# Weight sums of the in-projection on VectorE, the first tap of the convolution on ScalarE

## The reference

```python
zxbcdt = h @ in_w                                   # 1024 -> 5184 columns
z   = zxbcdt[..., :D_INNER]
xbc = jax.nn.silu(centred_dwconv(zxbcdt[..., D_INNER:D_INNER + CONV_DIM], conv_w, conv_b))   # 5 taps
dt  = jax.nn.softplus(dt_raw + dt_bias)             # 64 columns, two directions
cum = jnp.cumsum(dt_c * a_neg, axis=2)              # then the chunked scan of both directions
y   = rmsnorm((y_f + flip(y_b) + xs * d_skip) * jax.nn.silu(z), norm_w)
out = y @ out_w
```

## Time and profile before

| | us |
|---|---|
| median of 3 runs (lowest, highest) | 1460.6 (1460.18, 1460.69) |
| profiled execution, its own time | 1461.46 |
| its span in the trace | 1459.7 |
| TensorE busy in the span | 1343.7 (92%) |
| VectorE, ScalarE, GpSimd busy | 680.5, 409.2, 275.3 |
| DMA moved | 338.78 MB, mean 232 GB/s |

### The profile page before, as it was taken

The page is one execution under the profiler, slowest core; times in us unless marked ns, Lnnn a source line. Parts: engine busy times, 40 slices in busy tenths (PEclk is TensorE's granted clock), DMA queues, the critical chain, the costliest instruction groups (busy, mean ns, idle before and its releaser), DMA issues.

```text
span 1459.7 us, 30536 instructions
## 1 busy us (share of the span) xinstructions
PE 1343.7 (92%) x12917; PEld 917.8 (63%) x12917; DVE 680.5 (47%) x1154; ACT 409.2 (28%) x1032; POOL 275.3 (19%) x258
## 2 busy tenths in 40 slices
PE   5988989998999799999999999999999989999876
PEld 2466766676667688755566556688757855565432
DVE  4585988767776865651222222152363532221112
ACT  2312244454545310221222222222152302221111
POOL 0322352535265600000111111000000001111100
PEclk9999999999999999999999999999999989999988
DMA  9754344334531641525999999876321289999993
GB/s 346 283 173 144 116 143 147 129 132 145 202 117 37 181 129 60 208 110 184 396 397 389 383 378 381 349 253 219 108 106 53 81 305 363 392 395 398 401 406 144
DMA packets 132222, 338.78 MB, mean 232 GB/s; under 512 B 13363, under 2 KB 63339, under 8 KB 125803
## 3 DMA queue, kind: packets, MB, share of 16 engines
q1 hardware_dynamic: 122571, 313.38, 58.8%
q0 software_dynamic: 6208, 12.60, 2.5%
q10 hardware_dynamic: 3296, 10.73, 2.0%
HBM read 327.88 MB, written 16.91 MB: 236 GB/s over the span
## 4 chain that ended last, share of the span: by engine, by line
PE 64%; DMA 8%; DVE 7%; SPq 4%; issue 4%; ACT 2%; POOL 1%; DVEq 0%; ACTq 0%; POOLq 0%
PE ps L1852 14%; PE ps L1475 9%; PE ps L1891 7%; PE ps L1722 6%; PE ps L1782 4%; SPq L673 3%; DMA tmp<-in_moe_w_up 2%; PE ps L2181 2%; PE ps L1913 2%; PE ps L2091 2%; PE ps L1395 2%; DMA ssb<-in_moe_w_down 1%; PE ps L1551 1%; SPq L675 1%; DMA tmp<-in_shared_w_down 1%
## 5 line engine op out<-in xcount | busy, mean ns | idle before, releaser
L1852 PE MATMUL ps<-ring,ssb 128*32 128x256 f32 x2368 | 138.3, 386 | 6.5 <-DMA ring<-in_moe_w_up 6.5
L2786 DVE COPY big<-ps 32x256 f32<-32x256 f32 x162 | 68.6, 423 | 145.7 <-PE ps L1891 144.0
L2777 DVE TENSOR_TENSOR ssb<-ssb,ps 128x128 f32<-128x128 f32 (+1 forms) x56 | 19.5, 348 | 247.9 <-ACT ssb L1199 247.9
L1852 PEld LDWEIGHTS ps<-ring,ssb 128*32 128x32 f32 x2368 | 80.7, 112 | 58.9 <-DMA ring<-in_moe_w_up 9.9
L1475 PE MATMUL ps<-hT,own 128*128 128x256 f32 x456 | 109.6, 389 | 2.7 <-POOL own L861 2.6
L1475 PEld LDWEIGHTS ps<-hT,own 128*128 128x128 f32 x456 | 85.2, 193 | 25.1 <-issue 14.1
L1212 ACT COPY big<-ps 32x256 f32<-32x256 f32 x162 | 58.6, 362 | 141.1 <-PE ps L1891 139.6
L1852 PE MATMUL ps<-tmp,ssb 128*32 128x256 f32 x1568 | 88.7, 379 | 4.8 <-DMA tmp<-in_moe_w_up 4.7
L1199 ACT ACTIVATE ssb<-ps 128x128 f32<-128x128 f32 (+1 forms) x56 | 18.2, 324 | 249.3 <-PE ps L1852 249.3
L936 POOL DMA_INDIRECT y_rows<-big,sidx x32 | 30.0, 938 | 304.9 <-DVE big L2786 304.1
L2367 DVE SCALAR_TENSOR_TENSOR ring<-ring,par 128x512 f32<-128x512 f32 x96 | 85.6, 892 | 3.4
(11 more groups left out here) (463 smaller groups left out, 2429.0 us busy)
## 6 DMA issues: line engine op xcount, KB each, us to landing
ring<-in_ada_w SPq DMA_DIRECT2D x44, 1024.0 KB, 5.0
ring<-in_moe_w_gate SPq DMA_DIRECT2D x60, 512.0 KB, 12.4
ring<-in_moe_w_up SPq DMA_DIRECT2D x60, 512.0 KB, 16.0
ring<-in_moe_w_down SPq DMA_DIRECT2D x28, 1024.0 KB, 17.3
ring<-in_ssd_in_w SPq DMA_DIRECT2D x20, 1024.0 KB
tmp<-in_moe_w_down SPq DMA_DIRECT2D x20, 1024.0 KB, 17.5
tmp<-in_moe_w_gate SPq DMA_DIRECT2D x37, 512.0 KB, 12.5
tmp<-in_moe_w_up SPq DMA_DIRECT2D x37, 512.0 KB, 16.1
```

The source lines that it names most:

```text
L1852: ins = pe.matmul(tiled_gu[32 * c:32 * c + 32, 2 * h + i, :].rearrange("p (r n) -> p r n", r=2), XgT[l][:, k * C + 32 * g:k * C + 32 * g + ...
L2786: ins = dve.tensor_copy(Y[s % 2][32 * g:32 * g + 32, 256 * c:256 * c + 256], tiled_y[32 * c:32 * c + 32, 2 * h + i, :])
```

## The change

The weight sums go from GpSimd to VectorE, in two halves: s3 and s4 of pair i right behind the sum with r1 of that pair, s1 and s2 of pair i+1 right behind the sum with r5. The first tap of each conv goes from VectorE to ScalarE, for both chunks of a window behind the copy of r0. Softplus is cut in ten pieces that stand in windows 1 to 4, one behind each conv or silu; what follows from it (the logarithm of dt, the cumulative sums, their copies, transposes and split) comes about one window later, in pieces as well. `ada_rows(1)` stands ahead of the first conv of window 4. The copy of the dt products stands ahead of t1 to t4. In the tail, `activation_sums` come in two halves, the first four column blocks in pair 19 and no longer in pair 18.

```diff
...
-WEIGHTS_AT = {1: 10, 3: 11, 4: 12, 6: 13, 8: 14, 10: 15, 11: 16, 13: 17, 15: 18}
+FIRST_TAP_AT = {1: (2, 18), 5: (0, 20), 8: (2, 22)}
...
-            def mixed_weights(i):
...
-                if i > 1:
-                    pool.wait_ge(s_ip, product_made(i - 1, 3))
-                pool.tensor_tensor(b["s1"], b["a21"], b["a22"], ALU.add).then_inc(s_wm, 1)
-                pool.wait_ge(s_wm, done + 1)
-                pool.tensor_tensor(b["s2"], b["s1"], b["a11"], ALU.subtract).then_inc(s_wm, 1)
...
-                    pool.wait_ge(s_ip, product_made(i - 1, 5))
-                pool.wait_ge(s_wm, done + 2)
-                pool.tensor_tensor(b["s4"], b["a12"], b["s2"], ALU.subtract).then_inc(s_wm, 1)
...
-            for i in range(1, FIRST_STEP_PAIR):
-                mixed_weights(i)
...
-            mixed_weights(FIRST_STEP_PAIR)
...
-                if n in WEIGHTS_AT:
-                    mixed_weights(WEIGHTS_AT[n])
...
+            def conv_first_tap(i):
...
+                    act.wait_ge(s_pre, i + 1)
+                elif i % 2:
+                    act.wait_ge(s_ds, sum_made(pair, 4))
+                    act.wait_ge(s_pre, product_taken(pair, 6))
+                else:
+                    act.wait_ge(s_ds, sum_made(pair, 5))
+                if i >= 2:
+                    act.wait_ge(s_sil, i - 1)
+                act.activation(cacc[i % 2].rearrange("p (s n) -> p s n", s=2), pre[i % 2][:, :, 0:S], ACT.Identity,
+                               bias=par[:, 272 + ch:273 + ch], scale=par[:, ch:ch + 1]).then_inc(s_th, 1)
...
                 if w > 1:
                     take(w - 1, 6)
                 take(w, 0)
+                conv_first_tap(2 * w - 2)
+                conv_first_tap(2 * w - 1)
                 if w == 8:
                     act.wait_ge(s_ln, 2)
                     decay_exps(0, 0)
-                conv_tanh(2 * w - 2)
-                if w == 8:
                     decay_exps(0, 1)
                 take(w, 2)
+                conv_tanh(2 * w - 2)
...
-                elif w == 3:
+                elif w == 4:
+                    take_b(0)
                     act.wait_ge(s_sp, 8)
                     act.activation(lnd, dt[:, :, :].rearrange("p t n -> p (t n)"), ACT.Ln).then_inc(s_ln, 1)
-                elif w == 4:
-                    take_b(0)
+                elif w == 5:
                     decays()
...
             take(FIRST_STEP_PAIR - 1, 6)
+            conv_first_tap(16)
+            conv_first_tap(17)
             row_exps(0)
...
+                if FIRST_TAP_AT.get(n, (3, 0))[0] == 0:
+                    conv_first_tap(FIRST_TAP_AT[n][1])
+                    conv_first_tap(FIRST_TAP_AT[n][1] + 1)
...
+                if FIRST_TAP_AT.get(n, (3, 0))[0] == 2:
+                    conv_first_tap(FIRST_TAP_AT[n][1])
+                    conv_first_tap(FIRST_TAP_AT[n][1] + 1)
...
-                elif w == 5:
...
+                elif w == 5:
...
+            dve.wait_ge(s_bc, 16 * n_bc)
+            dve.wait_ge(s_sp, 1)
+            dve.tensor_copy(dtT, ps[:, 4, :]).then_inc(s_sp, 1)
...
+            def mixed_weights(i, first, last):
...
+                for n in range(first, last):
+                    to, x, y, op = (("s1", "a21", "a22", ALU.add), ("s2", "s1", "a11", ALU.subtract),
+                                    ("s3", "a11", "a21", ALU.subtract), ("s4", "a12", "s2", ALU.subtract))[n]
+                    if n == 0:
+                        arrived(dve, units[PAIR_ORDER[i][0]][PAIR_ORDER[i][1]])
+                    elif n == 1:
+                        dve.wait_ge(s_wm, 4 * (i - 1) + 1)
+                    elif n == 3:
+                        dve.wait_ge(s_wm, 4 * (i - 1) + 2)
+                    dve.tensor_tensor(b[to], b[x], b[y], op).then_inc(s_wm, 1)
+
+            mixed_weights(1, 0, 2)
...
+                elif part == 1:
                     dve.tensor_tensor(sp[1], sp[0], sp[7], ALU.max).then_inc(s_sp, 1)
-                elif part == 1:
+                elif part == 2:
...
+                elif part == 3:
                     link(dve.tensor_tensor(sp[4], sp[1], sp[3], ALU.mult))
                     link(dve.tensor_tensor(sp[5], sp[4], sp[4], ALU.mult))
-                elif part == 2:
                     link(dve.tensor_scalar(sp[2], sp[5], 1.0 / 17, None, ALU.mult))
-                    for n in (15, 13, 11, 9, 7, 5, 3):
+                elif part < 8:
+                    for n in ((15, 13), (11, 9), (7, 5), (3,))[part - 4]:
...
+            def spread_cum(d):
...
+            def split_cum(d, part):
...
+                if part == 0:
+                    dve.wait_ge(s_cT, 2)
...
                 dve.tensor_tensor(pair_output(i, odd, half), kept[first], ps[:, pair_bank(i, r), 0:S], ALU.add).then_inc(s_ds, 1)
+                if r == 1:
+                    mixed_weights(i, 2, 4)
+                elif r == 5 and i + 1 < len(PAIR_ORDER):
+                    mixed_weights(i + 1, 0, 2)
...
-                pair = PAIR_ORDER.index(("xbc", i // 2))
...
-                    dve.wait_ge(s_ds, sum_made(pair, 5))
-                if i >= 2:
-                    dve.wait_ge(s_sil, i - 1)
...
-                link(dve.tensor_scalar(o, pre[i % 2][:, :, 0:S], par[:, ch:ch + 1], par[:, 272 + ch:273 + ch],
-                                       ALU.mult, ALU.add))
+                dve.wait_ge(s_th, first_tap_made(i))
                 for tap in range(1, TAPS):
...
+            def activation_sums(i, part):
...
+                if part == 0:
+                    dve.wait_ge(s_yw, 2 * js[-1] + 2)
...
+                    return
...
             for w in range(1, FIRST_STEP_PAIR):
+                if w == 4:
+                    ada_rows(1)
                 conv(2 * w - 2)
-                if w in (2, 3):
-                    softplus({2: 1, 3: 3}[w])
-                elif w == 4:
+                if w in (2, 3, 4):
+                    softplus({2: 2, 3: 5, 4: 8}[w])
+                elif w == 5:
                     cum_copies()
-                elif w == 5:
+                elif w == 6:
                     dve.wait_ge(s_exps, 2)
                     dve.tensor_tensor(wdt[:, :, :], wdt[:, :, :], dt[:, :, :], ALU.mult).then_inc(s_wdt, 1)
...
                     dve.tensor_tensor(dt[:, :, :].rearrange("p t n -> p (t n)"), lnd,
                                       ncum[:, :, :].rearrange("p t n -> p (t n)"), ALU.add).then_inc(s_ln, 1)
-                elif w == 6:
-                    split_cum(1)
+                    modulation(1)
+                elif w == 7:
+                    split_cum(0, 1)
                 sum_product(w, 1)
                 if w == 8:
                     take_cb(0)
                 conv(2 * w - 1)
                 silu(2 * w - 2)
-                if w in (1, 2):
-                    softplus({1: 0, 2: 2}[w])
-                elif w == 4:
-                    ada_rows(1)
+                if w in (1, 2, 3, 4):
+                    softplus({1: 0, 2: 3, 3: 6, 4: 9}[w])
                 elif w == 5:
-                    split_cum(0)
+                    spread_cum(0)
+                elif w == 7:
+                    split_cum(1, 0)
                 sum_product(w, 4)
                 if w == 8:
                     take_state(0, 0)
                 silu(2 * w - 1)
-                if w == 5:
-                    modulation(1)
+                if w in (1, 2, 3):
+                    softplus({1: 1, 2: 4, 3: 7}[w])
+                elif w == 5:
+                    spread_cum(1)
+                elif w == 6:
+                    split_cum(0, 0)
+                elif w == 7:
+                    split_cum(1, 1)
                 sum_product(w, 5)
             mix(0, 0)
             take_state(0, 1)
@@ -2542,18 +2581,25 @@
                     modulation(n // 4 + 2)
             for j, i in enumerate(TAIL_PAIRS):
                 gate(10 + 2 * j)
+                if j:
+                    activation_sums(0, 0)
                 sum_product(i, 1)
                 gate(11 + 2 * j)
-                activation_sums(j)
+                if j:
+                    activation_sums(0, 1)
                 sum_product(i, 4)
                 sum_product(i, 5)
+            activation_sums(1, 0)
             for n in range(3):
                 weight_sum(0, n)
+            activation_sums(1, 1)
             gate(14)
             gate(15)
-            activation_sums(2)
+            for part in range(2):
+                activation_sums(2, part)
             weight_sum(0, 3)
-            activation_sums(3)
+            for part in range(2):
+                activation_sums(3, part)
```

64 lines of the change are left out of this document (26 added, 38 removed).

## The result

The changed kernel takes 1453.07 us in the median of 4 runs (1451.7 to 1454.31), the kernel before 1460.64 (1460.18 to 1462.89). The ratio is 0.9945, with a 95% interval of 0.9928 to 0.9962; timed again on another chip it is 0.9932 (0.9918 to 0.9945). So it is 8 to 10 us faster, not 24. The sign of the forecast was right, the size was two and a half to three times too large, and the time lies outside the range (1426 to 1451).

The account below looks back on a forecast made before the run. TensorE was taken to bound the kernel, waiting 33.3 us in the in-projection, mostly for VectorE slowed beside GpSimd and by order. Gains of 11.9 + 6.6 + 5.5 = 24.0 us off 1461.5 gave 1437 us, range 1426 to 1451.

Parts of the forecast that it names:

- Part 3, windows 2 to 7: In-projection, pairs 2 to 7: 100.1 us instead of 108.9, 8.8 less, with 11.7 us of new waits.
- The low clock that I had excluded: In pairs 2 to 7: no new wait over 2.5 us, so no low clock expected between 76 and 200 us.
- the chain over ScalarE: In the windows: r0, its copy, ScalarE's tap, conv taps, sum; r3 can start 6.4 us behind r0, plus the softplus piece.
- Part 3, window 8: From r0 of pair 8 to the first step: 20.3 us instead of 21.7, 1.4 less, and 1.7 of clock.
- Part 4, the steps: In the steps: 7.6 us of waits taken back, less 1.0 for two first taps in step 8; 6.6 us gained.
- I take 7.6 back: In the steps: 7.6 us of TensorE's waits for VectorE's states go, some of them too short for the list.
- Rival (c): In the steps: sums with r1 and r5 stand ahead of mix and states; 16 us slower, 1477 us; chance 0.05.
- Part 5, the tail: Pair 17 through the out-projection: 8.5 us gained with the clock, 3.0 lost at the out-projection's wait; 5.5 us net.
- Part 5, behind 516 us: Behind 516 us: loads follow the slots TensorE frees, so all moves along, with the same time there within 3 us.
- Rival (d): Behind 700 us: DMA engines are the bound (0.80 busy), so half the gain stays, 1449 us; chance 0.1.
- Part 1: Weight sums on VectorE: 76 instructions, 1.3 us for two, 2.6 us for a pair; the steps carry it.
- The price of the first tap: In the windows: about 0.7 us each on ScalarE; the price is its place behind the copy of r0, delaying the conv.

Follow-up runs that it names:

- The variant with the same code and 3.4 us of low clock: The changed kernel with whole activation sums back at their old places in pairs 18 and 19 (old tail): 1450.10 us, 0.9923 of the kernel before.
- order alone: The kernel before with only the reordering (softplus in ten pieces, row and cum copies moved), weight sums on GpSimd, old tail: 1458.13 us, 0.9979.
- sums alone: The kernel before with only the weight sums moved from GpSimd to VectorE: 1456.10 us, 0.9962.
- order and sums: The changed kernel without first taps on ScalarE and without the new tail: 1447.49 us, 0.9880 of the kernel before.
- the control: The kernel before, unchanged, timed and profiled once more: 1461.33 us, 1.0001 of the kernel before.

## Why the prediction was wrong

The gain came where it was forecast, in the windows, the steps and the tail. Most of its terms were too large, the waits taken back in the steps above all.

**Part 3, windows 2 to 7: right in total, partly by luck.** 101.5 us measured, 100.1 forecast; r3 of pair 2 at 8.8 us against 8.5; waits of at most 2.4 us, and the taps at 3.1. The waits stand where they were forecast, but they add up to 7.8 us and not 11.7. The low clock that I had excluded came once, 3.4 us long, in window 7, for 1.7 us. So without waits and low clock the windows take 92.0 us, and I had 88.4: two errors of nearly 4 us that cancel. What the forecast didn't ask is what stands there without the chain over ScalarE, which it worked out rightly at 6.4 us: with the tap back the windows take 95.0 us, with 3.6 us of waits.

**Part 3, window 8: wrong, 3.1 us.** I had less collision outweigh two and a half pairs of weight sums. The waits ahead of the first step add up to 3.7 us as before (0.7, 2.0, 1.0 against 1.3, 1.4, 1.0), and the clock fell there again.

**Part 4, the steps: wrong, 5.0 us.** "I take 7.6 back" of waits for states is the step that failed. They fell from 9.7 us behind the first step to 6.0, so 3.7 us, and TensorE's idle time in the steps fell from 16.9 to 12.6 us in all. The clock took most of it back: it was low for 10.2 us of the steps, before for 3.4, which costs 3.4 more. The variant with the same code and 3.4 us of low clock took 241.2, a gain of 4.5.

To see what made the gain, take half of the low-clock time in which TensorE worked off each profile's steps (an estimate, from the stage and the clock of the same trace). Then they take 244.0 us in all three profiles of the kernel before, with and without waits, 242.6 with order alone, 239.3 with sums alone, 240.0 with order and sums, 238.8 to 239.5 in the five profiles of the change and its like, and 240.0 to 240.1 with its first taps back. So the weight sums' move is worth 2.6 to 4.7 us there and the first taps some 0.8, where I had charged them 1.0. What kept the sums from giving more is partly their own length. There are 32 of them from 200 to 440 us, and they take more than the 0.65 us I gave them. Two groups of VectorE there, half of the weight sums and half of the mixes:

```profile
L2305 DVE TENSOR_TENSOR own<-ring 128x512 f32<-128x512 f32 x16 | 13.3, 829 | 0.0
...
L2443 DVE TENSOR_TENSOR ssb<-ssb,rstd 128x512 f32<-128x512 f32 x14 | 11.6, 828 | 0.5
```
The 32 sums are 26.2 us, 0.82 each. This half of the mixes fell from 1175 ns to 828, the other half from 1093 to 964, so the relief is there (the rule that I cited from the Trainium skill, GPSIMD Engine Reference, section 8, Key points, holds for them). VectorE is busy in 180.8 us of these 240, before 176.3: 26.2 us came, 4.3 of first taps went, and the other instructions shrank by some 17 us, for which I had 15. Rival (c) named the right danger, sums ahead of a state copy, and not the price: moving them behind it brought nothing.

**Part 5, the tail: wrong, 3.6 us.** 5.4 - 3.6 = 1.9 us measured, 8.5 - 3.0 = 5.5 forecast. The out-projection's wait was forecast at 4.6 and is 4.3. The rest is the first term: waits of 2.1 us came in pairs 18 and 19 for ScalarE's copies of products (L1001), which stand behind its tanh, squares and weightings; I hadn't followed them. What failed under both is a comparison: I set the new tail against the old one beside a busy GpSimd. Without it the old one loses 2.4 us and no clock there, and the new tail takes 3 us more.

**Part 5, behind 516 us: wrong, 3.8 us.** "So it all moves with it", from the loads that follow the slots. It did, against the control, up to the start of the second expert layer. 2.7 of the 3.6 us that are lost against it come at the late copy there, whose price over all profiles is 2.0 us; the rest is not explained. Rival (d) had a loss there for another reason, DMA, and the variants speak against it: the 6.5 us of the first tap in the windows are 6.6 by the ratios, and the 5.9 that the gates' order saves around the out-projection (7.5 less 1.6) are 6.0, so what was gained in front reached the end whole. I had looked at the order of VectorE's instructions and never at their number.

**Part 1 and the sum.** A weight sum takes 0.68 us in the median of all (L2305), against 0.65 taken, and 0.82 in the mean of the steps. The price of the first tap was placed rightly (0.76 us for one, behind the copy of r0) and left unquestioned as part of the sum: I never asked what the change would be without it. It costs 6.5 us.

## What to carry to other kernels

An edit that takes an engine's load off and one that spreads its long pieces can need each other; price them singly and together (here 5.6 and 3.1 us singly, 17.5 together, by the ratios on 1461 us). Moving an instruction to an idle engine is no gain if it comes between two steps of a chain that another engine waits on (here 6.5 us, and 20.5 with GpSimd busy): ask first how long the engine that is relieved will stand still. And of every place that an edit fills, ask what is queued behind it (the gates in the tail, the state copies in the steps).

## What was unexpected of the hardware

One instruction behind a branch of VectorE's program, untouched by the change and some 670 us behind the last one that it moves, starts 0.4 to 2.3 us late (1.6 in the change) or in time according to its number in the program: late at 1355 to 1401, in time at 1325 and below and at 1411 to 1413. Waits that do nothing, 20 to 116 of them, switch it on and off. When late, it starts 1.93 to 1.97 us behind the start of an 8 KB load of instructions, in eleven profiles of eleven.

The waits of TensorE of 2 to 3 us cost twice where the clock falls behind them, and whether it does isn't the same in each run of the same code (0.72 and 1.00 in the same 12 us). That also decides how finely a stage can be compared: sums alone looked no faster in the steps than the kernel before (246.7 against 245.7 us), with 3.9 us less idle time under 17 us of low clock. Of five profiles with the code of the change up to there, two had low clock behind the state copy of that wait and three had not.
